# The last pair's causal convolution moved out of the projection into the first tile of the delta rule, with the modulation sums and the first decay rows loaded earlier

## What is computed

```python
ada = silu(c) @ w_ada + b_ada            # 6 * 1024 modulation values
u = h * (1 + sc1) + sh1
proj = u @ w_in
qkv = silu(causal_depthwise_conv(qkv_a, conv_w))   # 3072 channels, 4 taps
q, k, v = split(qkv)                     # 8 heads of 128 each
g = -exp(a_log) * softplus(a_a + dt_bias)
o_a = gated_delta_rule(l2n(q), l2n(k), v, g, sigmoid(b_a))   # chunks of 64 tokens
y_b = window_attention(...)
merged = sig(gate_a) * y_a + sig(gate_b) * y_b
mix = merged @ w_out                     # then layer norm, then a mixture of experts
```

## Time and profile before

| what | value |
| --- | --- |
| median of 3 runs | 2023.97 us (2022.44 to 2028.07) |
| the profiled execution | 2027.32 us, span 2025.5 us |
| project | 301.7 to 600.2 us of the span |
| delta_rule | 600.2 to 914.8 us |
| TensorE busy in the span | 1828.3 us, 90% |
| mean granted TensorE clock | 0.959 of 2.4 GHz |

### The profile page before, as it was taken

One profiled execution on the slowest core, in us unless ns is written; L12 is line 12 of the kernel. 1 busy time (PEld: TensorE's weight loads), 2 busy tenths in 40 slices (PEclk: granted clock), 3 DMA queues, 4 the chain that ended last, 5 costly groups with the idle time before them and its releaser, 6 DMA issues. The chain is left out here.

```text
span 2025.5 us, 35243 instructions
## 1 busy us (share of the span) xinstructions
PE 1828.3 (90%) x14108; PEld 1037.0 (51%) x14108; DVE 1442.5 (71%) x1820; ACT 1063.9 (53%) x1290; POOL 357.2 (18%) x229
## 2 busy tenths in 40 slices
PE   4988869989969999998999999369999999999965
PEld 1655544434438999973444445344444444444432
DVE  5455555676867666735575768779999888888948
ACT  3455553245432333424333411159888888888944
POOL 0000000011101212110000000024444444444410
PEclk9999989989989999999999999579999999999988
DMA  8500007473364322106131322369999999999935
GB/s 316 100 22 22 1 5 287 156 268 107 115 194 107 86 59 63 35 2 200 53 104 53 115 73 73 135 249 410 403 404 410 404 393 401 394 391 392 384 133 209
DMA packets 161686, 391.32 MB, mean 193 GB/s; under 512 B 25340, under 2 KB 102773, under 8 KB 132880
## 3 DMA queue, kind: packets, MB, share of 16 engines
q1 hardware_dynamic: 146576, 357.87, 48.6%
q0 software_dynamic: 14976, 31.56, 4.1%
HBM read 361.68 MB, written 48.68 MB: 203 GB/s over the span
## 5 line engine op out<-in xcount | busy, mean ns | idle before, releaser
L2220 PE MATMUL ps<-w_gate_up_split,gathered_t 128*128 128x512 f16 x1728 | 387.6, 381 | 8.3 <-ACT gathered_t L2294 4.0
L2386 DVE SCALAR_TENSOR_TENSOR w_gate_up_split<-w_staged,w_gate_up_split 128x2048 f16<-128x2048 f32 x144 | 327.6, 2289 | 56.6 <-ACT w_gate_up_split L2285 55.1
L2285 ACT ACTIVATE w_gate_up_split<-w_staged 128x2048 f16<-128x2048 f32 x144 | 274.4, 1909 | 66.8 <-PEq L144 31.4
L2220 PEld LDWEIGHTS ps<-w_gate_up_split,gathered_t 128*128 128x128 f16 x1728 | 167.3, 98 | 209.0 <-ACT gathered_t L2294 10.5
L219 PE MATMUL ps<-u_transposed,w_gates_split 128*128 128x512 f16 x1152 | 254.3, 383 | 6.2 <-DVE merged_part L1744 3.1
L820 PE MATMUL ps<-u_transposed,w_dense_split 128*128 128x512 f16 x1152 | 252.5, 381 | 5.0 <-DVE w_dense_split L190 4.2
L2247 PE MATMUL ps<-w_down_split,hidden_t 128*128 128x512 f16 x864 | 193.8, 381 | 7.6 <-ACT hidden_t L2331 4.3
L219 PEld LDWEIGHTS ps<-u_transposed,w_gates_split 128*128 128x128 f16 x1152 | 113.3, 99 | 146.8 <-issue 14.6
L820 PEld LDWEIGHTS ps<-u_transposed,w_dense_split 128*128 128x128 f16 x1152 | 112.2, 98 | 148.2 <-issue 8.9
L2386 DVE SCALAR_TENSOR_TENSOR w_down_split<-w_staged,w_down_split 128x2048 f16<-128x2048 f32 x72 | 164.0, 2287 | 20.4 <-ACT w_down_split L2285 20.2
L2285 ACT ACTIVATE w_down_split<-w_staged 128x2048 f16<-128x2048 f32 x72 | 137.2, 1909 | 45.5 <-DMA w_staged<-in_w_down 29.3
(11 more groups left out here) (360 smaller groups left out, 2931.8 us busy)
## 6 DMA issues: line engine op xcount, KB each, us to landing
w_staged<-in_w_gate SPq DMA_DIRECT2D x72, 1024.0 KB, 12.1
w_staged<-in_w_up SPq DMA_DIRECT2D x72, 1024.0 KB
w_staged<-in_w_down SPq DMA_DIRECT2D x72, 1024.0 KB
w_dense_ring<-in_w_in SPq DMA_DIRECT2D x17, 1024.0 KB, 6.8
w_ada_ring<-in_w_ada SPq DMA_DIRECT2D x8, 2048.0 KB
w_gates_ring<-in_w_in SPq DMA_DIRECT2D x24, 512.0 KB, 6.4
qkv_scratch<-qkv_silu POOLq DMA_DIRECT2D x20, 512.0 KB, 3.5
attention_output<-qkv_scratch SPq DMA_DIRECT2D x8, 1024.0 KB, 5.9
```

The lines of the kernel that those rows point to most:

```text
L2220: last = pe.matmul(ps[:, GU[s] + j, :], xt[:, s, xp, k, :], w16[:, j, wp, k, :], start=(k == 0 and t == 0), stop=(k == KC - 1 and t == 2))
L2285: nc.scalar.activation(split(kind, 0, int(q)), staged(m, kind, int(q)), ACT.Identity, scale=W_SCALE).then_inc(hi_ok[kind + q], 1)
L2386: nc.vector.scalar_tensor_tensor(split(kind, 1, int(q)), staged(m, kind, int(q)), W_SCALE, split(kind, 0, int(q)), ALU.mult, ALU.subtract) ...
```

## The change

In project:

- The partial sum of piece 3 goes behind the convolution of pair 3. Pieces 4, 5 and 6 get their partial sums one pair sooner than theirs before (pairs 7, 8, 9), and piece 7 stands ahead of pair 10's convolution. Pieces 4 and 5 are both summed in `extras(8)`, 6 in `extras(9)`, 7 in `extras(10)`.
- The load of piece 6 stands at pair 10 of SyncE's list, ahead of `load_z(7)` and `load(11)`, and it and that of piece 7 wait for all square-sum stores, since their bias rows go to that buffer.
- The first residual tile is loaded after `load(2)`, and after a wait for the store of the attention output.
- ScalarE's exponentials of pair 10 come ahead of that pair's silu, and `key_scalars` follows pair 10's convolution.
- Pair 11 is copied and given its last tap, but its three other taps, its silu and its stores leave project.
- The decay rows of tile 0 are loaded at the end of project.

In delta_rule's tile 0:

- VectorE does the three passes of group 22 after `lower(0)`, and one of group 23 each before level 2, before level 3 and after level 3.
- ScalarE does the silus after level 1 and after level 4. SyncE stores both groups, waits for all late stores, then loads the values of tiles 0 and 1.
- `value_rows(0)` comes after level 5, and GpSimd's `queries(0)` waits for the copies of level 2.

Buffers are laid over others for it (`raw`, `acc`, `silu` and others over memory of the delta rule).

```diff
-    ADA_AT = {0: (0,), 1: (1,), 2: (2,), 3: (3,), 8: (4,), 9: (5,), 10: (6, 7)}
+    ADA_AT = {0: (0,), 1: (1,), 2: (2,), 3: (3,), 8: (4, 5), 9: (6,), 10: (7,)}
+    PARTIAL_AT = {0: 0, 1: 1, 2: 2, 7: 4, 8: 5, 9: 6, 10: 7}
...
                 if n >= 2:
                     sp.wait_ge(part_ok, n - 1)
-                    if n < LATE - 1:
+                    if n < 6:
                         sp.wait_ge(ada_out[n % 2], 16 * (n // 2))
+                    else:
+                        for b in range(2):
+                            sp.wait_ge(ssq_out[b], 64)
...
-            load_z(0)
             sp.dma_start(m.yb_dram.rearrange("n p t -> p n t"), m.yb[:]).then_inc(yb_out, 16)
             load_ada(1)
             for p in range(2, PAIRS):
                 load(p)
-                n = {4: 2, 5: 3, 6: 4, 7: 5, 11: 6}.get(p)
+                if p == 2:
+                    sp.wait_ge(yb_out, 16)
+                    load_z(0)
+                n = {4: 2, 5: 3, 6: 4, 7: 5, 10: 6}.get(p)
...
+            sp.wait_ge(gc_out, 16)
+            for half, rows_of in enumerate((slice(0, CHUNK), slice(CHUNK, P))):
+                sp.dma_start(m.gb[rows_of, 0], m.gc_dram.rearrange("(c h) x t -> c h x t", c=TC)[0:1, :, 0, rows_of].to_broadcast([CHUNK, H, CHUNK])
+                             ).then_inc(m.gb_in[0], 16)
             store_ada(6)
             store_ada(7)
...
-            sp.wait_ge(late_out, 16 * (2 * (PAIRS - POOLED) + 3))
...
-                if p in ADA_AT:
-                    partial(ADA_AT[p][0])
+                if p in PARTIAL_AT:
+                    partial(PARTIAL_AT[p])
                 if 2 <= p < 2 + TC:
                     residual(p - 2)
-                if p == 11:
-                    key_scalars()
-                convolve(p)
-                if p == 10:
-                    partial(LATE - 1)
+                if p < PAIRS - 1:
+                    convolve(p)
+                if p == 3:
+                    partial(3)
                 for n in ADA_AT.get(p - 1, ()):
                     row(n)
+                if p == 10:
+                    key_scalars()
...
             load_decays(0)
             load_decays(1)
+            for b in range(2):
+                sp.wait_ge(m.silu_ok, 2 * LAST_PAIR + b + 1)
+                sp.dma_start(m.qkv_dram[2 * LAST_PAIR + b], last_silu[:, b, :]).then_inc(m.late_out, 16)
+            sp.wait_ge(m.late_out, 16 * 6)
+            load_values(0)
             load_values(1)
...
-                value_rows(c)
+                if c >= 1:
+                    value_rows(c)
                 level(c, 5)
+                if c == 0:
+                    value_rows(c)
                 key_rows(c)
...
+            def last_rows(b):
+                act.wait_ge(m.conv_ok, 2 * LAST_PAIR + b + 1)
+                nc.scalar.activation(last_silu[:, b, :], acc[:, b, :], ACT.Silu).then_inc(m.silu_ok, 1)
...
                     level(c, k)
+                    if c == 0 and k in (1, 4):
+                        last_rows(k // 4)
...
+            def convolve_last(b, t):
+                n = 2 * LAST_PAIR + b
+                last = nc.vector.scalar_tensor_tensor(acc[:, b, :], raw[:, b, 1 + t:1 + t + T], conv[:, t, n:n + 1],
+                                                      acc[:, b, :], ALU.mult, ALU.add)
...
                 lower(c)
+                if c == 0:
+                    for t in range(3):
+                        convolve_last(0, t)
...
+                if c == 0:
+                    convolve_last(1, 0)
                 level(c, 2)
+                if c == 0:
+                    convolve_last(1, 1)
...
                 level(c, 3)
+                if c == 0:
+                    convolve_last(1, 2)
...
+            pool.wait_ge(S("n_ok"), 4)
             queries(0)
```

More of the change, by code:

```diff
@@ L715, in project @@
         part = m.sb("ada_partial_sums", [P, 2, 512], ctx=ctx)
[L716 to L719, removed]
+        ada_row = m.sb("ada_row_piece", [1, 2, 512], ctx=ctx)
+        rows = m.o[:, 6:8, :]
+        z = m.yb[:, 7, :].rearrange("p (h d) -> p h d", h=2)
+        spare = m.early_work[:, 2 * (4 + T):]
+        sc = spare[:, 0:512].rearrange("p (n c h) -> p n c h", n=8, c=TC)
         ea = m.sb("exp_a_log", [P, H], ctx=ctx)
         ssq_rows = m.sb("k_square_sums_rows", [TC * H, P], ctx=ctx)
-        gc_rows = m.sb("gc_rows", [TC * H, 2, P], ctx=ctx)
-        inv = m.sb("k_inverse_norms", [P, 2, TC, H], ctx=ctx)
+        gc_rows = spare[0:TC * H, 512:768].rearrange("p (n t) -> p n t", n=2)
+        inv = spare[:, 768:896].rearrange("p (n c h) -> p n c h", n=2, c=TC)
         eps = m.sb("norm_eps", [P, 1], ctx=ctx)
@@ L784, in store_ada @@
                 sp.wait_ge(ada_ok, n + 1)
[L785 to L801, removed]
+                sp.dma_start(ada_flat[:, 2 * D + n * 512:2 * D + (n + 1) * 512], row_piece(n)).then_inc(late_out, 16)
+            for b in range(2):
+                sp.wait_ge(silu_ok, 2 * POOLED + b + 1)
+                sp.dma_start(m.qkv_dram[2 * POOLED + b], silu[:, POOLED % 2, b, :]).then_inc(late_out, 16)
+            sp.wait_ge(gc_row_ok, 1)
+            sp.dma_start(m.gc_dram, gc_rows[:]).then_inc(gc_out, 16)
+            sp.wait_ge(yb_out, 16)
+            for b in range(2):
+                sp.wait_ge(stored[0][b], 64)
+                sp.wait_ge(stored[1][b], 64)
+            for c in range(2):
+                sp.dma_start(m.tiles[:, c, 0:2 * H], m.qkv_dram.rearrange("n p t -> p n t")[:, 0:2 * H, c * P:(c + 1) * P]).then_inc(m.tile_in[c], 16)
+            sp.wait_ge(gc_out, 16)
+            for half, rows_of in enumerate((slice(0, CHUNK), slice(CHUNK, P))):
+                sp.dma_start(m.gb[rows_of, 0], m.gc_dram.rearrange("(c h) x t -> c h x t", c=TC)[0:1, :, 0, rows_of].to_broadcast([CHUNK, H, CHUNK])
+                             ).then_inc(m.gb_in[0], 16)
             store_ada(6)
             store_ada(7)
-            sp.wait_ge(gc_out, 16)
             for b in range(2):
@@ L1105, in delta_rule @@
         qkv_in = m.tile_in
-        gb_in, eg_in = ([m.sem(f"delta_{n}_in{side}") for side in range(2)] for n in ("gb", "eg"))
+        gb_in, eg_in = m.gb_in, [m.sem(f"delta_eg_in{side}") for side in range(2)]
+        LAST_PAIR = 11
+        raw, acc = m.raw, m.o[:, 0:2, :]
+        last_silu = m.o[:, 4:6, :]
+        conv = m.vecs[:, VEC_N:].rearrange("p (t n) -> p t n", t=4)
         v_in = [m.sem(f"delta_v_in{side}") for side in range(2)]
@@ L1139, in load_decays @@
                     sp.wait_ge(S("qg_ok"), c - 1)
-                for s in range(2):
-                    sp.dma_start(gb[rows[s], c % 2], gc_view[c:c + 1, :, 0, rows[s]].to_broadcast([CHUNK, H, CHUNK])).then_inc(gb_in[c % 2], 16)
-                if c == 0:
-                    load_values(0)
+                if c >= 1:
+                    for s in range(2):
+                        sp.dma_start(gb[rows[s], c % 2], gc_view[c:c + 1, :, 0, rows[s]].to_broadcast([CHUNK, H, CHUNK])).then_inc(gb_in[c % 2], 16)
                 sp.dma_start(eg[:, c % 2], gc_view[c:c + 1, :, 1, :].to_broadcast([P, H, P])).then_inc(eg_in[c % 2], 16)
```

55 lines of the change are left out of this document (35 added, 20 removed).

## The result

The changed kernel takes 2012.31 us, the median of four runs (2011.88 to 2013.18), against 2025.94 for four runs of the kernel before. The ratio is 0.9928, with a 95% interval of 0.9911 to 0.9944: between 11 and 18 us faster. (The median before moved from 2023.97 to 2025.94 because a fourth run was added.) The forecast median was 2006.7 with a range of 2001 to 2015. The profiled execution took 2011.88 us with a span of 2010.0, 15.5 us less than the span before.

The account below looks back on a forecast made before the run. Project was taken as TensorE-bound except for some 22 us of stops, everything behind tile 0 as serial. Gains of 11.9 and 11.6 less 6.2 in tile 0 give 17.3 us: 2010.0 for the profiled execution, median 2006.7, range 2001 to 2015.

Parts of the forecast that it names:

- third rival: Tile 0: GpSimd's three instructions each block a VectorE instruction fully, 5.5 us where 2 allowed; gain 13.8, 2010.2 us; chance 0.12.
- fourth: Tile 0: values come late because the store or load is as slow as its slowest row; 9 us gained, 2015; chance 0.08.
- Pairs 3 to 5: Project: TensorE's stop at pair 5 closes, gain 10.6 us, plus 1.3 from the residual tile: 11.9 us by pair 6.
- first residual tile: Project: loaded after `load(2)`, for which ScalarE waited; worth 1.6 us, at least 0, taken as 1.3.
- Pair 11: Project: split weights end at 563.9, TensorE wants them at 565.1, 1.2 us to spare; the pair runs 0.95 late.
- End of project: Delta_rule begins at 588.6 instead of 600.2 on the old clock, gain 11.6 us; 23.5 us to here.
- The decay rows: Start of tile 0: VectorE need not wait for decays, 3.3 us sooner; last row lands at 589 to 590.
- The passes and GpSimd: Tile 0: last pass ends at 22.5 if nothing blocks, up to 25.8 if three VectorE instructions wait; taken as 24.5.
- The values: Tile 0: silu, store and load take 9.7 us behind the last pass; tile 1's similarities start at 36.25 instead of 31.06.
- slow clock behind the stop: Tile 0: after TensorE's stop for the values its granted clock stays lower, costing 0 to 2 us, taken as 1.
- second rival: Project: pair 5's stop isn't closed and a wait with slow clock returns; all 11.9 lost leave 5.4 us, 2018.6; chance 0.13.
- fifth: Project: `load(11)`, queued behind piece 6's load, comes late and stops TensorE; slower than before, 2031 us; chance 0.05.

Follow-up runs that it names:

- the early queries: Changed kernel without GpSimd's wait for the copies of level 2, so its queries and state scaling begin some 6 us into tile 0: 2015.43 us, ratio 0.9939.
- the two kernels where the pass ended some 2 us sooner: Changed kernel with GpSimd's first queries behind level 5's copies (2010.67 us), and changed kernel with decay rows stored and loaded before pair 10's stores (2011.12 us).

## Why the prediction was right, and where it was off

The forecast was a gain of 17.3 us for the profiled execution. The span shrank by 15.5, and from the start of project to the mark 22.96 - 7.11 = 15.85 us are won. The medians of the first comparison are 13.6 us apart. The forecast median of 2006.7 us was 5.6 too low, 2.0 of it from the median before. The measured 2012.31 lies between the 2010.2 of the third rival and the 2015 of the fourth, so the time alone doesn't pick out the forecast; the steps in the trace do. Their mechanism is as forecast, and most are a little too hopeful in size:

1. **Pairs 3 to 5.** Forecast 11.9 us by pair 6, measured 11.2 (446.19 - 301.73 against 436.50 - 303.27). The move of piece 3 was given 10.6 and brought 10.6 where it stands alone, with 1.6 us to spare at pair 5 where 1.7 were counted (410.5 and 412.15). The term that was too large is the first residual tile: 1.3 us were counted, but ScalarE's split in pair 1 comes only 0.2 us sooner in project, and by pair 4 TensorE is 0.5 us sooner. Why the 0.5 MB ahead of the load were worth so little no run shows; the forecast allowed that another transfer decides.
2. **Pair 11.** 1.2 us were to be spare; its split ends at 554.2 and TensorE wants it at 555.3. The wait of piece 6 for the sum of piece 4, which the forecast put on VectorE, is there (5.95 us).
3. **End of project.** To the start of delta_rule 23.5 us forecast, 23.0 measured; the difference is that of point 1.
4. **The decay rows.** Forecast 3.3 us, measured 1.8: they were issued before the block began, but had not landed when VectorE wanted them. SyncE's list holds them behind the stores of groups 20 and 21, which wait for their silu, so that their store goes out at 569.4 and their loads at 572.4; VectorE still waits 1.46 us. The forecast had put their landing at 589 to 590 on the clock of before, at most 1.4 us behind the block's start, and then counted no wait; VectorE had them at 2.65. With the decay rows issued 12 us sooner the wait is gone.
5. **The passes and GpSimd.** The last pass was put at 24.5 us, between 22.5 and 25.8, and ended at 25.9, just outside. The decays began 1.45 us later than counted, of which 0.9 were left when VectorE took level 1's first product (592.60, 13.8 us behind the start where 12.9 were forecast), and the hold-ups came to 2.5 us where 2 were counted. The mechanism of the third rival is there, but at two instructions instead of three and for less than half of its 5.5 us. Of the hold-ups before the change the forecast took back only the 0.94 us at the triangle; there were three, of 3.1 us together, but no wait of TensorE is put down to the other two. The Trainium skill's rule of the lock (page "SBUF — State Buffer", section "SBUF: two separate sides") fits all these traces: the VectorE instructions held up beside GpSimd's products all have two SBUF inputs, at whichever place the products stand, and those with one input in PSUM are not held up (0.41 us each at 597.3 to 598.3 in the changed kernel).
6. **The values.** The trip took 8.7 us where 9.7 were counted, and the slow clock behind the stop cost 1.5 us where 1 was. Tile 0 in sum 7.1 us instead of 6.2. The slow store and load of the fourth rival did not come: the load took 4.9 us, not 9.0.

The rest of the program passed the gain on: the first gather of the experts comes 15.3 us sooner (1309.3 against 1324.7), and 15.5 us arrive at the end. That this is so near to the 15.85 us is in part luck: project began 1.5 us later in the execution after, and the stretch behind the mark was 1.2 us shorter.

Against the second rival: no wait came back at pair 5. Against the fifth: `load(11)` was issued at 521.6 and its split was never late.

## What to carry to other kernels

When a list of edits moves the time, take each alone: here one line about an instruction that waited for a transfer ahead of work that was ready gave some 11 of 15 us, and the large edit that gives the change its name little. Work moved out of an idle end into a busy block brings a gain at the one place and a bill at the other, and the bill is the longest chain that hangs behind it: here a store and a load of data that lay in SBUF. Gains behind a common wait don't add up until that wait is gone. When two medians differ by more than an edit can explain, look in the traces at the stretches that the edit doesn't touch.

## What was not expected of the hardware

- The way of the two groups from the last pass to the values in SBUF took 8.7 and 8.8 us in the two profiles of the changed kernel, 9.0 with piece 3 put back and 9.2 with the early queries, where the pass ended 25.9 to 26.3 us behind the block's start. It took 9.4 and 9.9 us in the two kernels where the pass ended some 2 us sooner. The difference sits in the load (4.9 to 5.4 us against 5.65 and 6.1), not in the store. It ate part of two gains. The cause wasn't found.
- The same GpSimd work on the same tile held up VectorE by 3.1 us in the kernel before (three instructions, 0.94, 1.07 and 1.10) and by 0.5 us with piece 3 alone (one, 1.16 us instead of 0.68), by beginning 1 us later against VectorE's list.
- A GpSimd memset of 128x1024 at the start of the block (0.95 us) did not hold up VectorE's memset of the same size beside it (0.91 us, as without it). It was over before VectorE's first decay, so no run shows what it would do beside an instruction with two SBUF inputs.
